# A two-layer decoder trunk on one core: the expert loop turned by one step, with the next expert's first gate/up in this expert's last step

## What is computed

```python
def moe_ffn(hn, router, w_gate_up, w_down):
    logits = (hn @ router).astype(jnp.float32)
    top_v, top_i = lax.top_k(logits, TOP_K)
    w = jax.nn.softmax(top_v, axis=-1)
    gates = jnp.sum(jax.nn.one_hot(top_i, N_EXPERTS, dtype=jnp.float32) * w[..., None], axis=-2)
    gates = gates.astype(hn.dtype)
    out = jnp.zeros_like(hn)
    for e in range(N_EXPERTS):
        out = out + gates[..., e:e + 1] * swiglu(hn, w_gate_up[e], w_down[e])
    return out
```

## Time and profile before

| | |
|---|---|
| median of 3 runs | 1892.75 us (1892.37 to 1894.83) |
| profiled execution: its span, first to last instruction | 1892.9 us |
| busy: PE, DVE, ACT | 1694.2, 1352.8, 1084.9 us |
| mean granted clock of TensorE | 0.948 of full speed |
| transfers from HBM | 457.94 MB, 242 GB/s over the span |

### The profile page before, as it was taken

How to read it: one execution, slowest core, us unless ns; L and a number is a source line. 1 busy time by engine, 2 the same in 40 slices (tenths; PEclk the granted TensorE clock), 3 DMA queues, 4 the chain that set the end, 5 groups by cost and what they waited for, 6 DMA issues and landing times.

```text
span 1892.9 us, 21567 instructions
## 1 busy us (share of the span) xinstructions
PE 1694.2 (90%) x7672; PEld 1384.0 (73%) x7672; DVE 1352.8 (71%) x1387; ACT 1084.9 (57%) x1089; POOL 0.2 (0%) x4
## 2 busy tenths in 40 slices
PE   6998889997878686799899999998998998999986
PEld 5885768885658565688787787786886886877865
DVE  6645444555438363798898897897997987988964
ACT  5354333344434342676676676675776766766753
POOL 0000000000000000000000000000000000000000
PEclk9999889998888796899999999999999999999998
DMA  5552334553425104599798897897896996987922
GB/s 223 215 181 86 134 113 177 200 184 127 141 101 185 54 25 187 213 373 347 280 368 316 316 374 306 306 378 285 332 375 255 367 377 244 369 337 293 373 109 89
DMA packets 64077, 459.62 MB, mean 243 GB/s; under 512 B 7200, under 2 KB 7200, under 8 KB 8480
## 3 DMA queue, kind: packets, MB, share of 16 engines
q1 hardware_dynamic: 64032, 459.01, 64.5%
HBM read 457.94 MB, written 1.05 MB: 242 GB/s over the span
## 4 chain that ended last, share of the span: by engine, by line
PE 79%; DVE 11%; ACT 5%; issue 3%; DMA 1%; DVEq 0%; ACTq 0%; SPq 0%
PE banks L366 25%; PE banks L368 24%; PE banks L367 24%; DVE weights_low L1062 3%; ACT weights_high L744 2%; PE banks L439 2%; PE banks L414 1%; DMA raw_static<-static_dram 1%; PE banks L691 1%; PE banks L690 1%; DVE activations_t L1084 1%; DVE residual L1497 1%; ACT activations_t L770 1%; DVE scores_t L1385 0%; PE banks L609 0%
## 5 line engine op out<-in xcount | busy, mean ns | idle before, releaser
L1062 DVE TENSOR_TENSOR weights_low<-scratch,weights_high 128x2048 fp32r<-128x2048 f32 x336 | 761.5, 2289 | 114.8 <-ACT weights_high L744 114.7
L744 ACT ACTIVATE weights_high<-scratch 128x2048 fp32r<-128x2048 f32 x336 | 642.6, 1915 | 124.5 <-PE banks L368 124.4
L366 PE MATMUL banks<-weights_high,activations_t 128*128 128x512 f32 (+1 forms) x1568 | 628.3, 401 | 66.0 <-DVE weights_low L1062 49.8
L367 PE MATMUL banks<-weights_low,activations_t 128*128 128x512 f32 (+1 forms) x1568 | 614.2, 392 | 0.0
L368 PE MATMUL banks<-weights_high,activations_t 128*128 128x512 f32 (+1 forms) x1568 | 614.2, 392 | 0.0
L366 PEld LDWEIGHTS banks<-weights_high,activations_t 128*128 128x128 f32 x1568 | 301.7, 192 | 130.8 <-DVE weights_low L1062 32.4
L368 PEld LDWEIGHTS banks<-weights_high,activations_t 128*128 128x128 f32 x1568 | 301.3, 192 | 62.1
L367 PEld LDWEIGHTS banks<-weights_low,activations_t 128*128 128x128 f32 x1568 | 302.4, 193 | 56.6
L1062 DVE TENSOR_TENSOR weights_low<-raw_static,weights_high 128x2048 fp32r<-128x2048 f32 x99 | 221.8, 2257 | 123.3 <-ACT weights_high L744 121.8
L744 ACT ACTIVATE weights_high<-raw_static 128x2048 fp32r<-128x2048 f32 x99 | 185.1, 1892 | 122.6 <-PE banks L368 110.2
L366 PE MATMUL banks<-weights_high,hidden_t 128*128 128x512 f32 x536 | 214.3, 400 | 9.5 <-DVE hidden_t L1236 9.5
(11 more groups left out here) (226 smaller groups left out, 1026.2 us busy)
## 6 DMA issues: line engine op xcount, KB each, us to landing
scratch<-expert_dram SPq DMA_DIRECT2D x336, 1024.0 KB, 5.5
raw_static<-static_dram SPq DMA_DIRECT2D x97, 1024.0 KB, 4.9
consts_sb<-const_dram SPq DMA_DIRECT2D x1, 1058.0 KB, 6.9
residual<-x_dram SPq DMA_DIRECT2D x1, 1024.0 KB, 4.9
out_dram<-residual SPq DMA_DIRECT2D x2, 512.0 KB, 2.8
small_sb<-small_dram SPq DMA_DIRECT2D x1, 704.0 KB, 8.1
raw_static<-static_dram SPq DMA_DIRECT2D x2, 256.0 KB, 3.0
scratch<-gain_dram SPq DMA_DIRECT2D x1, 512.0 KB, 5.7
```

What stands on the lines that cost most here:

```text
L366: pe.matmul(oo, xh, wh, start=first, stop=False)
L367: pe.matmul(oo, xh, wl, start=False, stop=False)
L744: A(WH[:, slot, 0:w], raw[:, 0:w], ACT.Copy).then_inc(high_ready, 1)
L1062: V_.tensor_tensor(WL[:, slot, 0:w], raw[:, 0:w], WH[:, slot, 0:w].bitcast(F32), ALU.subtract).then_inc(low_ready, 1)
```

## The change

The loop's turn is moved by one step. PE in step n of a turn now does: first half of gate/up(n+1), transposes of hidden(n), second half of gate/up(n+1), down(n). In step 13 the gate/up is step 0 of the next expert. Step 0 of the first expert stands ahead of the loop; its two slabs are moved into the static stream, and each expert's slabs in HBM are put in the new order (`expert_turns`). The first turn (without scatters) and the last (without a next expert) are written out, so that `Fori` runs six times. The gather moves to step 11. x parts and y parts are made, counted and waited for by halves of 512 columns, and so are the adds to the residual. The scatters stay in steps 0 and 1, which are now one gate/up later. On DVE the low part of the natural x (L1466) and the split of the third slab go ahead of the router's arithmetic, and the third slab's high part on ACT too. SP loads the tail's first three slabs ahead of the last expert's. The clearing of the gate matrices (L1500, L1501) is gone. The dense feed-forward keeps its order and gets its own function.

```diff
-A_END = A_NOUT + 4
+A_FIRST = A_NOUT + 4
+A_END = A_FIRST + 2
...
+            def turn(at, first, last):
+                for n in range(ESTEPS):
+                    ahead = not (last and n == ESTEPS - 1)
+                    if ahead:
+                        pe.wait_ge(f_hid, at(ESTEPS, FSTEPS + n))
+                        if n == ESTEPS - 1:
+                            pe.wait_ge(e_xl, at(2, 3))
+                        gate_up(n + 1, 0, at(ESLABS, A_END + 3 * n), (A_END + 3 * n) % RW)
+                    hidden_t(n, 1, PS[:, 6 + n % 2, :], at(ESTEPS, FSTEPS + n + 1))
+                    if ahead:
+                        if n == ESTEPS - 1:
+                            pe.wait_ge(e_xl, at(2, 4))
+                        gate_up(n + 1, 1, at(ESLABS, A_END + 3 * n + 1), (A_END + 3 * n + 1) % RW)
+                    if n == 0 and not first:
+                        pe.wait_ge(e_yl, at(2, 0))
                         scatter(0)
...
+                    if n == 1 and not first:
+                        pe.wait_ge(e_add, at(4, -2))
                         scatter(1)
...
+                    if n == 11 and not last:
+                        pe.wait_ge(e_gtl, at(1, 1))
+                        gather(at(1, 2))
+                    pe.wait_ge(f_low, at(ESTEPS, FSTEPS + n + 1))
+                    j = 3 * n + 2 if ahead else 3 * n
+                    slab_mm(at(ESLABS, A_END + j), (A_END + j) % RW, range(2), D, [[PS[:, 0, :], PS[:, 1, :]]],
+                            lambda k: hidden_lhs(n, k, 1), n == 0, n == ESTEPS - 1)
...
+            gather(1)
+            for i in range(2):
+                pe.wait_ge(e_xl, 1 + i)
+                gate_up(0, i, A_FIRST + i, (A_FIRST + i) % RW)
+            turn(lambda m, c: c, True, False)
+            with pe.Fori(0, between, 1) as it:
+                turn(lambda m, c: it * m + (c + m), False, False)
+            turn(lambda m, c: between * m + (c + m), False, True)
...
+            def turn(at, i, first, last):
+                end = ESLABS - 3 if last else ESLABS + 2
+                for n in range(ESTEPS):
+                    f_t_low(n, 1, t_bank, at(ESTEPS, FSTEPS + n + 1))
+                    if n in (1, 2) and not first:
+                        expert_add(n - 1, 1, None)
...
+                    if n == ESTEPS - 2 and not last:
+                        x_low(0, at(2, 3))
+                    if 3 * n + 3 <= end:
+                        turn_low(3 * n + 3, at)
+                    if not (last and n == ESTEPS - 1):
+                        hidden(n + 1, at)
+                    if n == ESTEPS - 2 and not last:
+                        x_low(1, at(2, 4))
+                    if 3 * n + 4 <= end:
+                        turn_low(3 * n + 4, at)
+                    if n in (0, 1) and not first:
+                        expert_add(n, 0, at(2, n - 1))
```

More of the change, by code:

```diff
@@ L346, in _ @@
             with sp.If(rounds > 1):
-                with sp.Fori(0, NE, 1) as e:
-                    expert_slabs(e, (e + NE) * ESLABS)
-            done = rounds * (NE * ESLABS)
-            for s in range(A_END + RA, A_END + 6):
-                sp.wait_ge(low_ready, done + (s - RA + 1))
-                sp.dma_start(RAWA[:, s % RA, :], static[s, :, :]).then_inc(landA[s % RA], 16)
+                expert_slabs(NE - 1, (NE - 1) * ESLABS + A_END)
+                with sp.Fori(0, NE - 1, 1) as e:
+                    expert_slabs(e, (e + NE) * ESLABS + A_END)
+            for s in range(A_END, A_END + RA):
+                load(s, 512 if s == A_END else SLAB)
+            expert_slabs(NE - 1, rounds * (NE * ESLABS) + (A_END - ESLABS), last=True)
+            done = rounds * (NE * ESLABS) + (A_END - 2)
+            for i in range(RA, 6):
+                sp.wait_ge(low_ready, done + (i - RA + 1))
+                sp.dma_start(RAWA[:, (A_END + i) % RA, :], static[A_END + i, :, :]).then_inc(
+                    landA[(A_END + i) % RA], 16)
             for c in range(2):
@@ L862, in _, with f_sigmoid @@
             norm_t(1, T_NORM1)
-            def f_sigmoid(n, used, tiles, gu_bank, fbase):
+            def f_sigmoid(n, used, tiles, gu_bank, before):
                 act.wait_ge(slab_used, used)
-                if n:
-                    act.wait_ge(f_hid, fbase + n)
+                if before is not None:
+                    act.wait_ge(f_hid, before)
                 for tt in range(tiles):
@@ L1543, in _, with x_low, expert_add @@
-            y_low(turns + 1)
-            for tt in range(NT):
-                expert_add(tt, turns * 2 + (tt + 1))
-            dve.wait_ge(e_add, turns * 2 + 2)
+            def x_low(c, count):
+                dve.wait_ge(e_xh, count)
+                V_.tensor_tensor(XGL[:, 4 * c:4 * c + 4, :], PS[:, 4 + c, :].rearrange("p (k t) -> p k t", k=4),
+                                 XGH[:, 4 * c:4 * c + 4, :].bitcast(F32), ALU.subtract).then_inc(e_xl, 1)
+            def expert_add(tt, c, count):
+                if c == 0:
+                    dve.wait_ge(e_sc, count)
+                hh = h[:, tt, c * 512:(c + 1) * 512]
+                V_.tensor_tensor(hh, hh, PS[:, 4 + c, :], ALU.add).then_inc(e_add, 1)
@@ new lines, in _, with hidden, linked @@
+            gu_bank = lambda n, tt: PS[:, 2 + n % 2, :]
+            t_bank = lambda n: PS[:, 6 + n % 2, :]
+            def hidden(n, at):
+                def linked(m):
+                    m.then_inc(hid_step, 1)
+                    dve.wait_ge(hid_step, at(ESTEPS, n + 1))
+                f_hidden(n, at(ESTEPS, FSTEPS + n + 1), 1, gu_bank, linked)
+            select(0)
+            x_low(0, 1)
+            x_low(1, 2)
+            turn_low(1, before_first)
+            hidden(0, before_first)
@@ L1547, in _ @@
+            turn(lambda m, c: c, 0, True, False)
+            with dve.Fori(0, between, 1) as it:
+                turn(lambda m, c: it * m + (c + m), it + 1, False, False)
+            turn(lambda m, c: between * m + (c + m), between + 1, False, True)
+            for tt in range(NT):
+                for c in range(2):
+                    expert_add(tt, c, between * 2 + (tt + 3))
+            dve.wait_ge(e_add, between * 4 + 8)
             dve.sem_inc(h_ready, 2)
-            base = turns * ESLABS + A_END
+            base = between * ESLABS + (A_END + 2 * ESLABS - 2)
@@ L1589, in slabs_ffn, with expert_turns @@
     return np.stack(order)
+def expert_turns(slabs):
+    ahead = np.roll(slabs[:, 0:2], -1, axis=0)
+    return np.concatenate([slabs[:, 2:ESLABS - 1], ahead, slabs[:, ESLABS - 1:]], axis=1)
 def p_slab(p):
@@ L1614 @@
     w1 = a(nsa_cmp_w1)[0]
+    gu, dn = a(moe_w_gate_up)[0], a(moe_w_down)[0]
+    expert = np.stack([slabs_ffn(gu[e], dn[e]) for e in range(NE)])
     static = np.concatenate([
@@ L1640 @@
         "gain_dram": np.ascontiguousarray(np.broadcast_to(nf[1], (P, D))),
-        "static_dram": static, "expert_dram": expert,
+        "static_dram": static, "expert_dram": expert_turns(expert),
     }
```

313 lines of the change are left out of this document (137 added, 176 removed).

## The result

The change makes the kernel faster: **1809.38 us** (4 runs, 1804.69 to 1819.52) against 1892.56 us for the kernel before on the same chip (4 runs, 1892.06 to 1894.83). The ratio is 0.9561, 95% interval 0.954 to 0.9582. The forecast was 1815. The profiled execution is the shortest of the four: its own time is 1804.69 us, its span 1802.9, and its mean granted clock 0.964.

A forecast was written before the change was run, and what follows sets the result against it. PE, busy 90%, bounds the kernel. Entry 8.0, first turn 7.5, seven turns 58.0 and last turn 4.5 sum to 78.0 us saved, giving 1815 us; own range 1807 to 1822, with the first two rivals 1806 to 1834.

The forecast's parts named there:

- four waits: PE's idle times at each change of expert, 0.45, 1.01, 2.08 and 2.87 us, together 6.41, all to go.
- The ideal turn: Expert loop: one turn without the losses at the change of expert, 133.49 - 8.8 = 124.7, used as 124.8 us.
- the restart: Change of expert: each PE idle time also costs the last matmul's drain and a slow first one, some 0.2 us.
- a new wait of 0.6 to 0.7 us.: Once a turn near the change of expert, PE waits for DVE's next low split, ready T+11.85, wanted T+11.27.
- The margins: Around the change of expert: first slab's low split holds by 0.2 us, `scatter(1)`'s add by 0.3 to 0.4.
- the fourth wait: PE's 2.87 us before `scatter(1)`, to go with 36 matmuls instead of 24 between scatters, DVE adding by halves.
- Entry 8.0: Before expert 0: gate/up at 757.6 instead of 765.6 through splits done ahead and a gather 2.7 us earlier.
- First and last turn 7.5 + 4.5: First turn saves 7.5 us (no scatters, wait, half clock); last saves 4.5 (no ninth gather, shorter waits).
- The loop's back edge: Rival, 10%: the loop's back edge shows, 0 to 2.1 us for each of 7 passages; the middle gives 1823.
- Transfers do not set the pace: Rival, 3%: in the expert loop 326 GB/s is a ceiling, the turn stays at 133.8 us; 1873.
- The clock does not give way: Rival, 2%: granted clock falls in the experts under a load without pauses; at 0.90, 111 us more, 1926.
- Of the splits only the one forecast comes late: Rival, 15%: splits late at more places around the change of expert, 2.4 us more a turn; 1832.

The follow-up runs named there:

- the second set: The changed kernel run again with no edit, with a second profiled execution: 1815.04 us (5 runs, 1806.65 to 1818.05), ratio 0.9578.
- the two experiments: Two edits of the changed kernel: both half adds of a tile together again, 1810.44 us; the second scatter 12 matmuls earlier, 1837.36 us.
- x whole: Changed kernel with both halves of x copied and subtracted together behind the last step's hidden layer, TensorE waiting for both: 1817.83 us, ratio 0.9608.
- scatters near: Changed kernel with the second scatter 12 matmuls earlier, so 24 matmuls lie between the scatters as in the kernel before: 1837.36 us, ratio 0.9718.

## Why the prediction was right, point by point

The saving was to be 78.0 us and is 83.2 by the medians of the first set, 77.7 by those of the second; both times lie in the lower part of the range. Of the 5 us more in the first set, the traces give 3.9 to the turns and 1.1 to a half-clock stretch at the entry. That the second set's 1815.04 meets the forecast of 1815 is luck: the turns gave 3.9 us more than forecast there too, but its router came 1.9 us later than in the profile of before (746.07 against 744.18), and that profile is a run some 1.7 us over its median. (A run's time is 1.5 to 1.8 us more than its span; a run of the kernel before with the same span of 1892.9 took 1894.45 us. So the 0.15 us between span and median compared two different runs. The forecast, taken from the median, does not suffer by it.)

- **The four waits go, PE sets the pace.** Right. The ideal turn was 124.8 in the prediction; measured it is 124.94 less one wait of 0.24 and its restart of 0.24, 124.46. The step that was mis-sized is the restart, "some 0.2 us: 0.8". By the starts of the sample's matmuls the four restarts cost 0.16 to 0.30 us each, about 1.0 in all (distance of two starts, less the wait and what the matmul takes in a plain step): 133.49 - 6.41 - 1.0 - 1.6 = 124.5.
- **"a new wait of 0.6 to 0.7 us."** Right in place, at the split of the second slab ahead, and wrong in size: 0.24, with its restart 0.48. DVE's split ends at T+11.64, not 11.85 (T, the start of the last but one step's gate/up, is 1615.01 here). With the ideal turn, 0.34 too long, this makes 0.56 us a turn, 3.9 over seven, the largest error of the sum.
- **The margins.** The first slab's low part was to hold by 0.2 and has 0.27 (DVE ends it at 1620.86 + 2.29, PE wants it at 1623.42); `scatter(1)` was to hold by 0.3 to 0.4 and has 0.32. That the fourth wait went by the distance and not by the halves was said, and the two experiments show it.
- **Entry 8.0:** 7.91, with 2.60 from the gather (2.19 of it the natural x) and 5.31 from the splits: 3.98 are the order behind x, and 1.33 ACT's table load, which the prediction did not see at this place. The half-clock stretch that I left as it was is shorter, 9 matmuls instead of 14. By their starts it costs 1.9 us instead of 3.0: 1.1 of the 12.7 in the fourth line of the table. In the second profile it has 14 again, so this too is the clock's and not the change's.
- **First and last turn 7.5 + 4.5:** the rest of that line is 11.7, where 11.5 were forecast. The wait for y was to fall by 0.5 from 2.59; it is 2.01. The end of the changed kernel, where the next gains lay:

```profile
1751.25 0.50 PE L372 MATMUL banks<-activations_t,hidden_t 128*128 128x512 f32 x1 [2.01 <-DVE activations_t L1579]
...
1760.43 0.78 PE L372 MATMUL banks<-weights_high 128*128 128x512 f32 x1 [4.49 <-DVE weights_low L1097]
```

- **The rivals.** The loop's back edge costs nothing: turns inside the loop, into it and out of it all take 124.92 to 125.00 (the way out by `scatter(1)`, at 1522.91 and 1647.83). Transfers do not set the pace: the loop keeps it at 420 GB/s. The clock does not give way in 885 us with no pause over 0.35 us. Of the splits only the one forecast comes late, and `scatter(1)` has no wait.
- **What was not seen** is that the clock ahead of the experts changes from one execution to the next: 4.7 us of the difference of the profiles, and 6.6 of the 10.4 us between the two of the changed kernel.

## What to carry to other kernels

Where a loop's turn ends with a chain of small dependent steps, turn the loop by one step so that the next turn's independent work stands between them; what hides a wait is the work between the two ends of the chain, and it could be read off the trace in advance to a few tenths of a microsecond here. Compare kernels by intervals inside the trace that repeat (here the gathers, the same to 0.1 us in two executions of one kernel), since the whole varies by ten. A rate of transfer that a kernel shows is not a limit until it has been asked for more.

## What the runs showed of the hardware

- After a pause of PE the granted clock may fall to half for 6 to 8 matmuls of 512 columns. In the expert turns, counted in four traces: behind pauses of 1.17 to 1.20 us none of 7 times, of 2.06 to 2.12 us 3 of 14, of 2.32 to 2.33 us 4 of 7, of 2.87 to 2.90 us 16 of 16 (the kernel before in two executions, x whole, scatters near). Such a stretch costs some 1.6 us (129.13 less 127.55 with the scatters near). The length of the pause alone does not decide: behind the one of 3.01 to 3.04 us near the end of the program full clock follows in 7 of 12 traces. What decides is open.
- 420 GB/s from HBM for 600 us on one core, in transfers of 1 MB with 8 KB to a partition, beside PE, DVE and ACT at work, with the turn unchanged (124.95 us against 124.94).
- A step of the loop is 8.41 us long in some kernels' traces and 8.43 in others', with the same instructions on PE and no wait in it; the cause is open.
